# First block: the heads of chunk 0 turned in chunk 2 instead of chunk 1, and the attention's first step one piece later

## The reference, cut to what matters

```python
for l in range(DEPTH):                     # 2
    h  = rms_norm(x, norm_g[l]) * (1 + sc[:, None]) + sh[:, None]
    hc = rms_norm(ctx, norm_g[l]) * (1 + sc_c) + sh_c
    qa, ka, va, ga, qb, kb, vb, gb, qn, kn, vn, gn = split_proj(h @ w_in[l])
    ... # the same of hc
    qa = axial_rope(rms_norm(qa.reshape(b, s, A_HEADS, 2, A_DK), diff_q_norm[l]), row, col)
    ka = axial_rope(rms_norm(ka.reshape(b, s, A_HEADS, 2, A_DK), diff_k_norm[l]), row, col)
    ... # qb, kb as qa, ka; qn, kn without the rotation
    oa = map_query_blocks(lambda q_blk: diff_attend(q_blk, ka_all, va_all, lam), qa)
    ... # two more kinds of attention, gates
    x = x + gt[:, None] * (jnp.concatenate([ya, yb, yn], axis=-1) @ w_out[l])
```

## Time and profile before

| what | value |
|---|---|
| median of 3 runs | 1265.45 us (1265.17 to 1270.0) |
| the profiled execution | 1265.86 us, its span 1264.1 us |
| mean granted clock of TensorE | 0.953 |
| busy: PE, DVE, ACT, POOL | 1146.9, 725.0, 601.8, 257.7 us |
| the chain that ended last, by engine | PE 70%, DVE 10%, ACT 7%, POOL 5%, issue 4%, DMA 2% |

### The profile page before, as it was taken

How to read it: one execution, slowest core, us unless ns; L and a number is a source line. 1 busy time by engine, 2 the same in 40 slices (tenths; PEclk the granted TensorE clock), 3 DMA queues, 4 the chain that set the end, 5 groups by cost and what they waited for, 6 DMA issues and landing times.

```text
span 1264.1 us, 16703 instructions
## 1 busy us (share of the span) xinstructions
PE 1146.9 (91%) x5877; PEld 911.9 (72%) x5877; DVE 725.0 (57%) x1322; ACT 601.8 (48%) x1174; POOL 257.7 (20%) x324
## 2 busy tenths in 40 slices
PE   5979799898989978999998998989799999999987
PEld 2656577676668766778777786878678887888875
DVE  3467777777763653644455566564465545565543
ACT  3333454435762443564574553444444445544553
POOL 1482330354005131302300112000022101121100
PEclk8988899899999998899999999999899999999999
DMA  9745364324112223122202764553355665344301
GB/s 334 139 153 177 105 152 134 106 94 131 39 66 85 86 68 92 59 83 67 84 18 92 267 195 151 167 180 134 117 171 180 190 186 156 117 126 125 117 1 51
DMA packets 79001, 157.92 MB, mean 125 GB/s; under 512 B 5760, under 2 KB 6056, under 8 KB 78664
## 3 DMA queue, kind: packets, MB, share of 16 engines
q1 hardware_dynamic: 75592, 147.41, 36.9%
q0 software_dynamic: 3328, 9.46, 3.3%
HBM read 153.73 MB, written 3.11 MB: 124 GB/s over the span
## 4 chain that ended last, share of the span: by engine, by line
PE 70%; DVE 10%; ACT 7%; POOL 5%; issue 4%; DMA 2%; SPq 0%; ACTq 0%; POOLq 0%; DVEq 0%
PE bank L720 17%; PE bank L722 16%; PE bank L721 16%; PE bank L869 4%; PE bank L844 3%; PE bank L854 3%; POOL small L1439 3%; PE bank L947 2%; DVE w_lo L1629 2%; DVE work L1649 2%; PE bank L920 2%; ACT w_hi L1044 2%; PE bank L932 1%; PE bank L740 1%; POOL stage L503 1%
## 5 line engine op out<-in xcount | busy, mean ns | idle before, releaser
L720 PE MATMUL bank<-w_lo,h_hi 128*128 128x512 f32 (+1 forms) x1152 | 465.2, 404 | 26.0 <-DVE h_lo L1698 9.9
L722 PE MATMUL bank<-w_hi,h_hi 128*128 128x512 f32 (+1 forms) x1152 | 449.5, 390 | 0.0
L721 PE MATMUL bank<-w_hi,h_lo 128*128 128x512 f32 (+1 forms) x1152 | 448.9, 390 | 0.0
L1629 DVE TENSOR_TENSOR w_lo<-raw,w_hi 128x1024 fp32r<-128x1024 f32 x224 | 286.7, 1286 | 192.8 <-ACT w_hi L1044 191.6
L1044 ACT ACTIVATE w_hi<-raw 128x1024 fp32r<-128x1024 f32 x224 | 235.9, 1057 | 293.2 <-PE bank L722 249.9
L720 PEld LDWEIGHTS bank<-w_lo,h_hi 128*128 128x128 f32 x1152 | 224.6, 195 | 77.7 <-issue 29.2
L722 PEld LDWEIGHTS bank<-w_hi,h_hi 128*128 128x128 f32 x1152 | 222.8, 193 | 45.4
L721 PEld LDWEIGHTS bank<-w_hi,h_lo 128*128 128x128 f32 x1152 | 224.5, 195 | 40.2 <-issue 0.2
L869 PE MATMUL bank<-work,stage 128*128 128x128 f32 x640 | 93.8, 288 | 0.0
L1617 POOL TENSOR_TENSOR stage<-stage 128x512 f32<-128x512 f32 x24 | 42.3, 1786 | 217.7 <-DVE stage L503 217.7
L869 PEld LDWEIGHTS bank<-work,stage 128*128 128x128 f32 x640 | 84.6, 203 | 1.0 <-issue 0.2
(11 more groups left out here) (172 smaller groups left out, 1097.9 us busy)
## 6 DMA issues: line engine op xcount, KB each, us to landing
raw<-in_b_w_in_dram SPq DMA_DIRECT2D x80, 512.0 KB, 3.6
raw<-in_w_in_dram SPq DMA_DIRECT2D x56, 512.0 KB, 3.9
raw<-in_a_w_in_dram SPq DMA_DIRECT2D x48, 512.0 KB, 4.3
raw<-in_w_ada_dram SPq DMA_DIRECT2D x32, 512.0 KB, 3.7
work<-in_w_ada_dram SPq DMA_DIRECT2D x16, 512.0 KB, 11.5
raw<-in_w_out_dram SPq DMA_DIRECT2D x16, 512.0 KB, 3.5
raw<-in_a_w_out_dram SPq DMA_DIRECT2D x16, 512.0 KB, 3.5
raw<-in_b_w_out_dram SPq DMA_DIRECT2D x8, 512.0 KB, 3.5
```

The costliest lines, as they stand in the source:

```text
L720: pe.matmul(bank, hT(h_hi, ph, kt, tt), w_lo[:, s, k, lo:lo + w], start=first, stop=False)
L721: pe.matmul(bank, hT(h_lo, ph, kt, tt), w_hi[:, s, k, lo:lo + w], start=False, stop=False)
L722: mm = pe.matmul(bank, hT(h_hi, ph, kt, tt), w_hi[:, s, k, lo:lo + w], start=False, stop=last)
L1629: dve.tensor_tensor(w_lo[:, i % SPLIT, :, :], raw[:, PIECE_AT[p] % RAW, :, :], w_hi[:, i % SPLIT, :, :].bitcast(F32), ALU.subtract).then_i ...
```

## The change

`turned_at` takes the place of the table for in0 and in1 in chunks 1 and 2: nothing is turned in chunk 1; tile 0 and 1 of chunk 0 are turned in piece (2, 0), tile 2 and 3 in piece (2, 1). From chunk 3 on, and in din, the table stands as before. The two engines that used the table, PE in two places and ACT, now ask the function. `FIRST_BESIDE` is (2, 2) for in0 and in1, so `solo` goes from 19 to 18 in both, and one step more is done after the last piece.

```diff
+def turned_at(ph, c, n, k):
+
+    if ph == "din" or c > 2:
+        return (c - 1, TURNED_AFTER[(n, k)]) if c and (n, k) in TURNED_AFTER else None
+    return (0, 2 * n + k) if c == 2 and n < 2 else None
...
-FIRST_BESIDE = {"in0": (2, 1), "in1": (2, 1), "din": (11, 1)}
+FIRST_BESIDE = {"in0": (2, 2), "in1": (2, 2), "din": (11, 1)}
...
                                 for k in range(2):
                                     product(ph, c, p, k, tt)
-                                if tt % 2 and c and (n, tt // 2) in TURNED_AFTER:
-                                    head_turn(ph, c - 1, TURNED_AFTER[(n, tt // 2)])
+                                if tt % 2 and turned_at(ph, c, n, tt // 2):
+                                    head_turn(ph, *turned_at(ph, c, n, tt // 2))
...
-                    tt = TURNED_AFTER.get((n, k))
-                    if c and tt in tts:
-                        head_turn(ph, c - 1, tt)
+                    at = turned_at(ph, c, n, k)
+                    if at and at[1] in tts:
+                        head_turn(ph, *at)
...
-                        if c and TURNED_AFTER.get((n, 0)) in tts:
-                            turned_heads(ph, c - 1, TURNED_AFTER[(n, 0)])
+                        at = [turned_at(ph, c, n, k) for k in range(2)]
+                        if at[0] and at[0][1] in tts:
+                            turned_heads(ph, *at[0])
...
-                        if c and n < pairs - 1 and TURNED_AFTER.get((n, 1)) in tts:
-                            turned_heads(ph, c - 1, TURNED_AFTER[(n, 1)])
+                        if n < pairs - 1 and at[1] and at[1][1] in tts:
+                            turned_heads(ph, *at[1])
...
-                                    lambda: turned_heads(ph, c - 1, TURNED_AFTER[(n, 1)]) if c else None)
+                                    lambda: turned_heads(ph, *at[1]) if at[1] and at[1][1] in tts else None)
```

## The result

The changed kernel takes **1272.63 us** (median of 20 runs, 1268.10 to 1278.65), the kernel before beside it 1269.04 (20 runs, 1265.17 to 1270.18). The ratio is **1.0033**, 95% interval [1.0022, 1.0043]: slower by 4 us, where 4 us faster was forecast, and 6 us above the top of the range. The profiled executions have spans of 1266.9 and 1264.1 us.

A forecast was written before the change was run, and what follows sets the result against it. It took PE, busy 91% of the span, as the bound, so only its waits could be won. Layer 0 at +2.0 and layer 1 at -5.8 us summed to -3.8, giving 1262.0 us, range 1256.5 to 1266.5.

The forecast's parts named there:

- The waits, layer 0: Layer 0, chunk 2: PE waits 5.8 us at (2, 0) and 4 us before the total, both set by ACT's emptying order.
- the 6.8 us: Layer 0, chunk 1: PE's waits before tiles 0 and 1 (3.35 and 3.42 us), of which nothing is gained.
- Layer 1 through its projection: Layer 1 up to its last piece: shorter waits and one step fewer bring the end 7.5 us earlier.
- The wait ahead of the third turned tile: Layer 1, piece (2, 1): a new 2.4 us wait for ACT's copy of tile 1, then 2 us of low clock.
- The moved step: Behind each layer's projection: one attention step more, costing 1.9 us, partly covering a wait already there.
- +1.9 - 0.9 + 0.9 + 0.7: Layer 0: moved step 1.9, covered wait -0.9, two turned tiles sharing bank 6 0.9, totals ahead of tiles 0.7 us.
- +1.9 - 1.1 + 0.9: Layer 1: moved step 1.9, covering 1.1 of the 1.88 us wait at 632.12, shared bank 0.9 us.
- 0.4 to 3 us: Both ends for the moved step outside the projection, per layer; the low end because table load and fill are there anyway.
- Its own sign of being wrong: Prediction is wrong if, among other signs, the steps behind the projection take over 3 us more.
- The table load itself: ACT, both layers: 1.28 us by the profile row; 2.66 us with drain would make the sum 0.6 us worse.
- The ends of the unknown: Total's speed, low-clock length and moved step left open: layer 0 between -2 and +4.5, layer 1 between -8 and -3 us.
- the rival that ended on that side: Layer 1, chunk 2: the load of (3, 0) lands about 6 us later, nothing is won: 1267 to 1268 us; chance 0.09.

The follow-up runs named there:

- e4: Changed kernel, with ACT copying the second turned tile ahead of its split in pieces (2, 0) and (2, 1): 1268.76 us, ratio 1.0010 to the kernel before.
- e11: The changed kernel itself, unaltered, run again on the same chip as the kernel with both repairs: 1274.17 us, ratio 1.0050 to the kernel before.
- e7: Changed kernel, with the attention's first step back behind (2, 1) and ACT's copy of a turned tile ahead of its split: 1259.17 us, ratio 0.9939.
- e1: Changed kernel with FIRST_BESIDE back at (2, 1), so only the turns are moved: 1264.33 us against 1269.37, ratio 0.9976.

## Why the prediction was wrong

- **The waits, layer 0: right.** Foretold 5.8 us at (2, 0), 4 ahead of the total, the total from 106.5 to 109.1, the scores of step 0 near 122, PE's wait for DVE ending at 152.2, 0.6 early at the last piece. Measured 6.75, 3.54, 107.38 to 110.14, 122.63, 151.86, and 0.8 early. That ACT's copies stand behind its splits, and that nothing of the 6.8 us is won here, was the mechanism (`e4`).
- **Layer 1 through its projection: right, a little small.** Foretold 7.5 us, measured 8.3. The wait ahead of the third turned tile was 2.79 (foretold 2.4), but no low clock followed it (granted 1.00 below). The scores of step 0 came at 497.54, which is 491.3 less the 6.2 us that layer 1 started late, where 493.8 was forecast: 2.5 better, 2 of it the low clock that did not come. Of these 2.5 us 1.7 were gone again by the end of the projection, so the closeness of 7.5 and 8.3 is in part luck.
- **The moved step: the step that failed.** "+1.9 - 0.9 + 0.9 + 0.7" in layer 0 and "+1.9 - 1.1 + 0.9" in layer 1, with "0.4 to 3 us" as its ends, measured **+7.2 and +4.8** in the changed kernel and the same in the step alone. (Its own sign of being wrong, steps behind the projection that take over 3 us more, is what came.) The sum came out at -3.8 and the profiled executions differ by +2.8 in span, a miss of 6.6; this term alone is 12.0 where it had 4.3, 7.7 more, and layer 1's larger gain gives 1 back. Three things were wrong in it. It priced the step by its matmuls and let it "cover" the wait of 0.91 at the last piece; the cover became the wait of 5.74. It looked at PE's order there and not at DVE's, where four products stand behind the step's output. And it said that table load and fill "are there anyway": they are, but before no fresh step's exponential waited behind the load.
- **The table load itself: as the row had it.** ACT's load at 288.31 takes 1.28 us, and the exponential starts at 289.60. The Trainium skill, "ScalarE: Activation LUTs", section "What ACT_TABLE_LOAD costs", counts 2.66 us for a switch with its drain, by which PE would have waited 0.6 us at (2, 0) in layer 1. It did not wait there. In the trace the exponential starts 0.01 us behind the end of the load, so the time by the row holds here, and no run shows the drain.
- **The ends of the unknown** were taken from PE's rows alone, so both were too low, and "slower" had no case that came from there: the rival that ended on that side was a DMA in chunk 2, which did not occur.
- With both orders repaired the change is 0.9966, 4 us faster, which is what was forecast, but by other means. The kernels with the step behind (2, 1) are at 0.9934 and 0.9939: repaired, the moved step still costs some 3 us (the intervals overlap). The forecast had less than 1 for the same thing, its terms of 4.3 behind the projections less the 1.8 and 1.7 us that one step fewer saves inside them.

## What to carry to other kernels

A step moved behind the last piece of a matmul phase is not priced by its matmuls: follow its whole chain (maximum, table load, exponential, output), and on each engine in that chain read what is queued *behind* it. A wait that goes because another stands in its place is no gain until the engine's next orders have been read too; here two swaps of order on ACT and DVE were worth 8 to 10 us, more than the change itself. When a total waits for products, moving the total doesn't help if the products stay: move them into idle time of the engine that makes them.

## What the hardware did that was not expected

One program gave, with the same waits, granted clocks that differ. The changed kernel stops for 0.48 us ahead of a total of w_ada, near 188 us, in the execution profiled first and in the one of `e11`. Windows around it, first execution:

```profile
187.00:192.00 5.00, 4.54 (x34) 1.00 0.44 141
192.00:198.00 6.00, 6.00 (x29) 1.00 0.41 147
```

and `e11`:

```profile
188.00:193.00 5.00, 4.52 (x23) 0.76 0.36 97
193.00:199.00 6.00, 6.00 (x25) 0.63 0.26 97
```

Behind the same wait the clock stayed at its upper level (2.4 GHz) in one and was at the lower one (1.2 GHz) for part of 11 us in the other. The two spans are 1266.9 and 1275.7 us, with no instruction changed. The Trainium skill, "TensorE: Matmul & The Clock Gate", section "Part 1: The HAM clock gate (the "warmup" mystery)", says that the gate's watching runs free of the kernel, so that one kernel comes out differently from run to run. These two executions did come out differently; that this is the reason, they do not show. That is why a single profiled time says little here, and why the stretches above are compared and not the places in the span; a stretch is not free of it either (58.74 and 60.71 in `e7` and `e1`). Nor does the length of a wait alone decide it: behind the wait of 2.24 us at 118.50 the kernel before ran at 0.50, behind the longer 2.79 us of the changed kernel's layer 1 the clock stayed up, and behind its 6.75 us of layer 0 it was at 0.50. Windows of the changed kernel at the last two:

```profile
94.00:100.00 6.00, 5.37 (x13) 0.50 0.71 200
...
487.80:493.00 5.20, 2.41 (x15) 1.00 0.86 258
```
